# Expert loops of a two-block model: row fetches before the wait for a step's results, results brought back by quarters of the width on two queues

## The reference

```python
def hier_moe(h, w_group, b_group, w_expert, b_expert, w1, w3, w2):
    ...
    expert_id = g_idx * MOE_EXPERTS_PER_GROUP + e_idx          # 2 of 32 experts per token
    combine = jnp.sum(jax.nn.one_hot(expert_id, MOE_EXPERTS, dtype=jnp.float32) * weights[..., None], axis=1)
    hid = jax.nn.silu(jnp.einsum('td,edf->tef', t, w1)) * jnp.einsum('td,edf->tef', t, w3)
    hid = hid * combine.astype(hid.dtype)[:, :, None]
    y = jnp.einsum('tef,efd->td', hid, w2)                     # d = 1024, f = 128
    return y.reshape(b, s, d)

# first_block, at the end of each layer
        x = x + gate2[:, None, :] * ffn
# first_block then norms x; in layer 1 a Mamba mixer comes next, then a second mixture; second_block follows
```

## Time and profile before

| | |
|---|---|
| median of 3 runs | 3735.78 us (3733.54 to 3743.85) |
| profiled execution | 3733.54 us, span 3731.7 us |
| TensorE busy | 3389.3 us, 91% of the span |
| VectorE, ScalarE, GpSimd busy | 43%, 22%, 3% |
| mean granted TensorE clock | 0.96 |
| DMA | 393.79 MB, mean 106 GB/s |
| expert loop of layer 0, of layer 1 | about 365 to 578 us, 1237 to 1444 us |

### The profile page before, as it was taken

How to read it: one execution, slowest core, us unless ns; L and a number is a source line. 1 busy time by engine, 2 the same in 40 slices (tenths; PEclk the granted TensorE clock), 3 DMA queues, 4 the chain that set the end, 5 groups by cost and what they waited for, 6 DMA issues and landing times.

```text
span 3731.7 us, 33495 instructions
## 1 busy us (share of the span) xinstructions
PE 3389.3 (91%) x12600; PEld 1925.0 (52%) x12600; DVE 1619.1 (43%) x2969; ACT 832.1 (22%) x1646; POOL 129.1 (3%) x132
## 2 busy tenths in 40 slices
PE   7987877999998776988899999999989789999998
PEld 3443443444443443554455555555554446687776
DVE  1153224555542223776633444222348764453334
ACT  2141112223321112116223121111120423221112
POOL 0000220000000221000000000000000000000000
PEclk9998998999999898999899999999999999999999
DMA  7634673676423574110111111111222011222222
GB/s 245 206 86 157 256 280 121 189 228 200 127 60 136 209 292 158 41 34 1 40 43 45 46 51 51 57 57 51 66 59 65 14 56 51 56 71 83 83 81 68
DMA packets 404493, 393.79 MB, mean 106 GB/s; under 512 B 27728, under 2 KB 345296, under 8 KB 395632
## 3 DMA queue, kind: packets, MB, share of 16 engines
q1 hardware_dynamic: 375008, 352.20, 29.6%
q0 software_dynamic: 18432, 19.98, 1.7%
q10 hardware_dynamic: 10896, 19.48, 1.6%
HBM read 440.78 MB, written 31.52 MB: 127 GB/s over the span
## 4 chain that ended last, share of the span: by engine, by line
PE 75%; DVE 8%; DMA 6%; ACT 3%; issue 2%; POOL 0%; SPq 0%; DVEq 0%; ACTq 0%; POOLq 0%
PE psum L637 31%; PE psum L622 24%; DMA arena<-h_dram,pair_u 5%; DVE arena L1831 3%; PE psum L1016 3%; PE psum L843 2%; PE psum L824 2%; PE psum L720 1%; ACT arena L1326 1%; DVE arena L1824 1%; PE psum L691 1%; PE psum L809 1%; PE psum L1143 1%; PE psum L1155 1%; PE psum L985 1%
## 5 line engine op out<-in xcount | busy, mean ns | idle before, releaser
L622 PE MATMUL psum<-hT,ring 128*128 128x512 f32 (+1 forms) x1920 | 778.1, 564 | 15.2 <-DVE hT L1824 12.9
L637 PE MATMUL psum<-hT,ring 128*128 128x384 f32 (+1 forms) x2176 | 624.6, 440 | 4.2 <-DVE arena L1831 4.2
L637 PE MATMUL psum<-arena,ring 128*128 128x384 f32 (+1 forms) x2080 | 596.7, 440 | 17.9 <-ACT part_sum L1334 16.4
L622 PEld LDWEIGHTS psum<-hT,ring 128*128 128x128 f32 x1920 | 365.0, 192 | 423.2 <-issue 408.4
L637 PEld LDWEIGHTS psum<-hT,ring 128*128 128x128 f32 x2176 | 414.8, 191 | 197.0 <-issue 20.2
L637 PEld LDWEIGHTS psum<-arena,ring 128*128 128x128 f32 x2080 | 396.6, 191 | 196.7 <-ACT part_sum L1334 18.5
L1334 ACT ACTIVATE arena<-psum 128x512 f32<-128x512 f32 (+5 forms) x481 | 207.9, 466 | 666.8 <-PE psum L622 288.4
L622 PE MATMUL psum<-arena,ring 128*128 128x512 f32 (+1 forms) x896 | 336.5, 531 | 0.0
L1831 DVE SCALAR_TENSOR_TENSOR arena<-arena,psum 128x128 f32<-128x128 f32 (+3 forms) x264 | 123.9, 475 | 484.7 <-PE psum L622 268.9
L1828 DVE TENSOR_TENSOR ring<-ring 128x512 f32<-128x512 f32 x304 | 202.4, 687 | 286.9 <-PE psum L637 275.8
L1334 ACT ACTIVATE part_sum<-psum 128x384 f32<-128x384 f32 (+1 forms) x228 | 100.9, 443 | 870.1 <-PE psum L637 866.2
(11 more groups left out here) (203 smaller groups left out, 2668.4 us busy)
## 6 DMA issues: line engine op xcount, KB each, us to landing
arena<-in_moe_w SPq DMA_DIRECT2D x64, 1536.0 KB, 11.5
ring<-in_w_in SPq DMA_DIRECT2D x172, 512.0 KB, 3.9
ring<-in_ada_w SPq DMA_DIRECT2D x96, 512.0 KB, 5.5
ring<-in_ssm_w_in SPq DMA_DIRECT2D x48, 512.0 KB, 6.6
ring<-in_w_mod SPq DMA_DIRECT2D x48, 512.0 KB, 4.9
ring<-in_w_branch SPq DMA_DIRECT2D x64, 256.0 KB, 3.1
ring<-in_mix_w_in SPq DMA_DIRECT2D x16, 512.0 KB, 7.7
arena<-y_dram SPq DMA_DIRECT2D x16, 512.0 KB, 7.1
```

Source lines behind the costliest of these rows:

```text
L622: mm = nc.tensor.matmul(b[:, 0:n], ws[k // 8][0][:, k % 8, :], rhs(k)[:, o:o + n], start=(k == 0), stop=(k == nk - 1))
L637: mm = nc.tensor.matmul(flat(bank_, nb), lhs[:, k, :], rhs(k), start=(start and k == 0), stop=(k == 3), skip_group_check=True)
```

## The change

In GpSimd's program the fetches of places 3 and 4 go out before the loop, and each turn fetches place i+5, still ahead of the wait for the result of place i. The return is cut by quarters of the width (256 columns, 1 KB per piece, all 512 tokens): SP brings the first pair's quarters, ScalarE's queue the second pair's. VectorE adds a quarter as it lands and takes up the transposed blocks of the quarter before; TensorE waits per quarter and not for all four.

```diff
+        def y_quarter(l, c, q):
+            return y_dram[l][S * c:S * c + S, 2 * P * q:2 * P * q + 2 * P].rearrange("(t p) n -> p t n", p=P)
...
 # TensorE
-                for t in range(4):
-                    eng.wait_ge(vector_done, pe.at(("y_tok", l, t)))
                 for k in range(KD):
+                    eng.wait_ge(vector_done, pe.at(("y_tok", l, k // 2)))
...
 # SP
+                eng.wait_ge(tensor_done, sp.at(("step_done", l, ORDER[-1])))
                 for i in range(STEPS - DEEP, STEPS):
                     eng.wait_ge(y_stored[i % DEEP], sp.at(("y_out", l, i)))
-                eng.wait_ge(tensor_done, sp.at(("step_done", l, ORDER[-1])))
-                for t in range(4):
-                    for c in range(2):
-                        r0 = S * c + P * t
-                        eng.dma_start(y_tok[c][:, t, :], y_dram[l][r0:r0 + P, :]).then_inc(y_back_landed[t], 16)
+                for q in range(4):
+                    eng.dma_start(y_tok[0][:, :, 2 * P * q:2 * P * q + 2 * P], y_quarter(l, 0, q)).then_inc(y_back_landed[q], 16)
...
 # ScalarE
+                for i in range(STEPS - DEEP, STEPS):
+                    eng.wait_ge(y_stored[i % DEEP], ac.at(("y_out", l, i)))
+                for q in range(4):
+                    eng.dma_start(y_tok[1][:, :, 2 * P * q:2 * P * q + 2 * P], y_quarter(l, 1, q)).then_inc(y_back_landed[q], 16)
...
 # VectorE
-                for t in range(4):
-                    eng.wait_ge(y_back_landed[t], 32 * (l + 1))
-                    tt(y_tok[0][:, t, :], y_tok[0][:, t, :], y_tok[1][:, t, :], ALU.add).then_inc(vector_done, ve.step(("y_tok", l, t)))
-                for k in range(KD):
-                    b, free = full("moe_y", l, k)
-                    stt(xT[:, k, :], b, M(l, 5, k), xT[:, k, :], ALU.mult, ALU.add).then_inc(vector_done, ve.step([free, ("x", loop, k)]))
+                for q in range(5):
+                    if q < 4:
+                        eng.wait_ge(y_back_landed[q], 32 * (l + 1))
+                        part = [t[:, :, 2 * P * q:2 * P * q + 2 * P] for t in y_tok]
+                        tt(part[0], part[0], part[1], ALU.add).then_inc(vector_done, ve.step(("y_tok", l, q)))
+                    if q:
+                        for k in (2 * q - 2, 2 * q - 1):
+                            b, free = full("moe_y", l, k)
+                            stt(xT[:, k, :], b, M(l, 5, k), xT[:, k, :], ALU.mult, ALU.add).then_inc(vector_done, ve.step([free, ("x", loop, k)]))
...
 # GpSimd
                 spare(0)
+                fetch(DEEP)
+                fetch(DEEP + 1)
                 for i in range(STEPS):
                     s, q = ORDER[i], i % DEEP
-                    if i + DEEP < STEPS:
-                        fetch(i + DEEP)
+                    if i + DEEP + 2 < STEPS:
+                        fetch(i + DEEP + 2)
                     eng.wait_ge(vector_done, po.at(("y_rows", l, i)))
```

## The result

| | before | changed |
|---|---|---|
| median | 3739.13 us of 4 (3733.54 to 3743.85) | 3684.83 us of 4 (3675.32 to 3688.86) |
| profiled execution, span | 3733.54, 3731.7 | 3688.29, 3686.5 |

The ratio is 0.9852, with a 95% interval of 0.9825 to 0.9878: 54 us less, where 34 were forecast.

A forecast was written before the change was run, and what follows sets the result against it. TensorE's chain bounds the kernel nearly everywhere, so only its idle can give time. From 3733.5, 32 us for the loops' groups and 2 for the return give 3699.5, said as 3700; range 3674 to 3726, chance 0.75.

The forecast's parts named there:

- The fetches: Row fetches in the expert loop, issued two scatters sooner: the 4.62 us wait before the transposes goes, scatters aren't delayed.
- C: Weights transfer issued when step b ends, needed by the next step b; forecast as the next wait, 2.5 us.
- The size of a group: Three steps of the expert loop, two static and one spare; 27.25 us before in the mean, fourteen groups.
- C until T + 17.0: TensorE waits for C's landing before the second static up; T is the end of step a's down.
- The clock's 1.5 a group: TensorE at the slow clock after a wait in each group, 1.5 us; the low bound has none, saving 53 us.
- The edge between 1.98 and 2.38 us: Other groups' waits before the next up-projection, 1.98 and 2.38 us; the forecast wait of 2.5 was placed there.
- a's scatter: Scatter of a, the first static step (b the second, c spare); the late fetch was issued right behind it.
- A: Weights transfer issued when step a ends, needed by the next step a; forecast wait about 1.6 us.
- The spare weights: Spare step's weights on GpSimd's queue, issued near T + 17, landing near T + 25; forecast to cost nothing.
- my rival: Spare weights behind the next weights land at T' + 16.6 (T' the next T): +141 us, 3875; chance 0.07.
- The cover of 4.1 us: Waits after the spare step, 1.6 for A and 2.5 for C, said to cover a late spare up.
- The return: After the expert loop, by quarters on two queues: net -0.9 us a layer, -2 for both.

The follow-up runs named there:

- fetch_only: The kernel before with only GpSimd's part of the diff, the moved fetches; the return stays as before. Measured 3684.66, ratio 0.9854.
- return_only: The changed kernel with the fetches put back where they were, so only the return by quarters on two queues is new. Measured 3739.75, ratio 0.9997.
- short_weights: The changed kernel with the down weights, the last third of the columns, left out of every weights transfer but the first five. Measured 3638.61, ratio 0.9721.
- fetch_dropped: The changed kernel with the fetches' limit at row 1, so nearly all their rows are dropped. Measured 3668.45, ratio 0.9808.
- one_ahead: The changed kernel with each fetch one place ahead of the original, not two: one fetch before the loop, place i+4 in turn i. Measured 3670.13, ratio 0.9816.
- spare_late: The changed kernel with spare weights issued one step later, behind the scatter of the next static step. Measured 3847.23, ratio 1.029.
- one_queue: The changed kernel with all eight quarters of the return issued from SP. Measured 3679.63, ratio 0.9841.
- one_ahead_warm: The changed kernel with fetches one place ahead and the return's transposes done twice for the first three quarters. Measured 3668.23, ratio 0.9809.
- one_ahead_half: The changed kernel with fetches one place ahead and one half of the spare steps' down done twice. Measured 3676.67, ratio 0.9829.
- one_ahead_both: The changed kernel with fetches one place ahead, half of the spare steps' down done twice and the first three quarters' return transposes doubled. Measured 3674.12, ratio 0.9819.

## Why the prediction was right, and what was mis-sized

- **The fetches.** As predicted, the wait before L809 (now L813) went to nothing, the scatters weren't delayed, and a wait for C took its place. fetch_only shows that this is the whole gain, return_only that the old wait comes back without it, short_weights that it is the weights that TensorE now waits for. The cause given, weights in flight beside the fetch, was read from 13.2 us for a fetch, which moves rows, and 2.1 for spare weights, of which nearly all rows are dropped, so the two aren't of one kind. The same trace has the fair pair: the fetch issued at 403.14, in the empty stretch, landed in 4.4 us, the one at 406.98 in 13.2. Both are for a static step; from issue to landing, windows at 403.14 and at 406.98:

```profile
arena<-h_dram,pair_u POOLq DMA_INDIRECT x1, 4.4
...
arena<-h_dram,pair_u POOLq DMA_INDIRECT x1, 13.2
```

- **The size of a group** was forecast at 24.95 and measured at 23.9. Two terms were too large and one was too small. "C until T + 17.0" measured 16.1 in the mean of fourteen. The clock's 1.5 a group measured 14.8 / 14 = 1.06: eight ups of fourteen were slow, most by 1.69 as in the earlier trace rows, six weren't. In three more profiles of the same loop it was 0.6 to 1.4. The edge between 1.98 and 2.38 us, at which the prediction placed its 2.5, isn't one: in the trace before already a wait of 2.04 us was followed by 5.36 and one of 2.10 by 3.67. Against that, a step that starts out of a wait takes 6.68 from its up to the end of its down (446.16 to 452.84), not the 6.45 of steps in a row: 16.1 + 6.68 + 1.06 = 23.84. Over fourteen groups that is 47.5 us saved for 32. What was called step 21 in reading the groups is the step at place 21; the seven groups are right.
- **Why C came sooner** wasn't settled by one run. The fetches' bytes beside the weights account for 0.3 to 0.5 us (fetch_dropped, and about 0.5 in one_ahead). That no fetch starts right behind a's scatter any more, beside A (406.98 in the earlier trace rows, T + 2.3; now the first behind it is at 409.79, T + 5.1), would go the same way: the up that needs A started at T + 7.0, a wait of 0.6 us, not at 8.0, a wait of 1.6. This is argued only.
- **The spare weights** cost nearly nothing, as forecast: three weight loads of TensorE waited for them in layer 0, 1.5 us in all. The trace of the changed kernel doesn't give their landing; in fetch_dropped it was 3.4 us in the median of layer 0, at most 3.9, where 5 to 8 were forecast. spare_late shows the price beside the next weights. It put the spare up at T' + 11.2 where my rival had T' + 16.6: two transfers beside weights were priced as two heavy ones, and with nearly all rows dropped they took 8.5 us. The cover of 4.1 us was wrong the other way. b's down stands behind the spare up, so C comes later by what the spare up waits, and A's wait is 0.6 us: nearly nothing is covered. The two errors nearly cancel (12.5 us a group over the forecast one; the six groups touched in layer 0 measured 35.9, 12.0 over the changed kernel's 23.9), so that 3847 came near 3875 is partly luck. For the forecast itself the cover was not needed.
- **The return** was forecast at -2 us and measured at -2.4 in the profile and nothing in the timed runs. Its terms, measured in layer 0 (forecast in brackets): start of the last add +1.56 (+1.3), from there to the sums 3.05 (3.5), slow sums +1.24 (+1). one_queue shows that the second queue gives nothing, one_ahead_warm that the slow transposes and sums come from the idle during the return.
- **What would have shown otherwise.** Of the signs named, ups on the ring's weights never waited 4 us, and C never came in the mean later than T + 18.5. Downs were 24 us apart, near the 25. The idle before L828 grew less than from 1.7 to 4 us a group, to 42.0 / 14 = 3.0, and four fifths of it, not half, stand before the second static step. Fetches and scatters landed in 10.5 us (median), 11.6 at most, where 10 to 20 were forecast.

Open: why with half a filling the wait went from C to A in layer 0 (one_ahead_half, and in part one_ahead_both), and why groups of one kernel differ by up to 1 us between layers and executions (23.4 / 24.4 and 23.75 / 23.3), most of which is the number of slow ups.

## What to carry to other kernels

When a transfer is late because others share the engines, issue it earlier only as far as it needs, and ask which transfer is waited for next: here one place ahead removed the same wait as two, and the weights came 0.5 us sooner. A small transfer on a queue of its own is not small beside large ones, so it should go out ahead of them, in the stretch in which the engines are empty. Before you count a later wait as cover for a delay, ask whether what it waits for was started by the step that is delayed; then it moves along and covers nothing. And a wait that moves may cost less than its length says, or more, by what the engine behind it does at the lower clock.

## What the runs showed of the hardware

- Two gathers of which nearly all rows are dropped landed in 2.1 us alone and in 8.5 (median) beside weights of 1536 KB.
- A fetch of a static step landed in 4.4 us when it was issued in the empty stretch (403.14, before) and in 13.2 beside weights (406.98); a scatter in 2.5 (399.20) and about 10 to 12.
- A short idle is followed by a slow up in some cases and not in others, and its length alone doesn't decide: after 3.24 us the up took 3.67 (granted clock 1.00, the level of 2.4 GHz), after 2.92 us 5.35 (granted clock 0.67 in the mean, 0.50 at its start, the level of 1.2). Counted over all loops of all profiles here (without the second of spare_late): of 64 waits of 1.2 to 1.9 us before an up none was followed by a slow one, of 94 of 1.9 to 3.5 us 47 were, and all three longer ones.
- The same 4.19 MB in pieces of 1 KB needed 14.8 us to the last add, in pieces of 4 KB 13.3; whether one queue issued them or two made no difference (14.85, 14.82). The next weights ran beside the end of both.
- Identical code ahead of the first loop ended at 364.16 and 357.25 in two executions of one kernel: of 7 us in a profile one execution says nothing.
